# MLA scores from split fp32r operands instead of fp32 products, with the splitting placed two heads ahead

## The reference

```python
q_pe = apply_rope(q_pe, cos[:, :, None], sin[:, :, None])
k_pe = apply_rope(k_rope, cos, sin)
scale = (MLA_NOPE + MLA_ROPE) ** -0.5
...
s = (jnp.einsum('bqhd,bkhd->bhqk', qn, k_nope)
     + jnp.einsum('bqhd,bkd->bhqk', qp, k_pe)).astype(jnp.float32) * scale
...
p = masked_softmax(s, kpos[None, :] <= qpos[:, None])
return jnp.einsum('bhqk,bkhd->bqhd', p.astype(v.dtype), v)
```

## Time and profile before

| | |
|---|---|
| median of 3 runs | 1079.6 us (1079.23 to 1080.19) |
| the profiled execution's own time | 1080.06 us |
| its span | 1078.0 us |
| TensorE busy | 1058.9 us, 98% |
| VectorE busy | 634.5 us, 59% |
| ScalarE busy | 500.1 us, 46% |
| GpSimd busy | 101.7 us, 9% |

### The profile page before, as it was taken

The page is one execution under the profiler, slowest core; times in us unless marked ns, Lnnn a source line. Parts: engine busy times, 40 slices in busy tenths (PEclk is TensorE's granted clock), DMA queues, the critical chain, the costliest instruction groups (busy, mean ns, idle before and its releaser), DMA issues.

```text
span 1078.0 us, 14561 instructions
## 1 busy us (share of the span) xinstructions
PE 1058.9 (98%) x5706; PEld 906.8 (84%) x5706; DVE 634.5 (59%) x795; ACT 500.1 (46%) x620; POOL 101.7 (9%) x163
## 2 busy tenths in 40 slices
PE   8999999999999999999999999999999999999996
PEld 7889898888877888888888888888888888888885
DVE  4655765788765645556556545555655545655565
ACT  4646644776664544334334333433433433443434
POOL 2145100532203000000000000000000000000003
PEclk9999999999999999999999999999999999999999
DMA  9586562252335465655666656566666655656552
GB/s 332 165 209 198 180 211 85 73 196 78 94 103 157 157 195 179 191 182 192 192 195 195 188 187 186 183 192 192 195 194 189 189 183 185 191 192 195 194 196 78
DMA packets 89138, 190.44 MB, mean 177 GB/s; under 512 B 8758, under 2 KB 29836, under 8 KB 88716
## 3 DMA queue, kind: packets, MB, share of 16 engines
q1 hardware_dynamic: 88668, 189.41, 55.3%
q10 hardware_dynamic: 432, 0.52, 0.2%
HBM read 187.82 MB, written 2.10 MB: 176 GB/s over the span
## 4 chain that ended last, share of the span: by engine, by line
PE 92%; DVE 3%; ACT 2%; issue 1%; POOL 1%; DMA 0%; DVEq 0%; ACTq 0%
PE ps L1660 22%; PE ps L1266 14%; PE ps L1267 14%; PE ps L1270 14%; PE ps L1663 11%; PE ps L1533 2%; PE ps L1534 1%; PE ps L1537 1%; PE ps L1517 1%; PE ps L1492 1%; DVE w_lo L831 1%; PE ps L1331 1%; PE ps L1471 1%; PE ps L1518 1%; ACT w_hi L559 1%
## 5 line engine op out<-in xcount | busy, mean ns | idle before, releaser
L831 DVE TENSOR_TENSOR w_lo<-raw,w_hi 128x2048 fp32r<-128x2048 f32 (+4 forms) x198 | 402.6, 2036 | 354.7 <-ACT w_hi L566 287.8
L566 ACT ACTIVATE w_hi<-raw 128x2048 fp32r<-128x2048 f32 x119 | 228.1, 1917 | 396.3 <-PE ps L1270 200.8
L1660 PE MATMUL ps<-xT,w_hi 128*128 128x512 f32 x1024 | 279.5, 394 | 1.3 <-DVE h_sb L1035 1.0
L1660 PEld LDWEIGHTS ps<-xT,w_hi 128*128 128x128 f32 x1024 | 175.9, 189 | 26.1 <-issue 1.3
L1663 PEld LDWEIGHTS ps<-xT,w_lo 128*128 128x128 f32 x1024 | 157.1, 189 | 21.7
L1266 PE MATMUL ps<-w_hi,hidT 128*128 128x512 f32 x448 | 174.5, 390 | 0.0
L1267 PE MATMUL ps<-w_lo,hidT 128*128 128x512 f32 x448 | 174.4, 389 | 0.0
L1663 PE MATMUL ps<-xT,w_lo 128*128 128x256 f32 x1024 | 162.8, 281 | 0.0
L1270 PE MATMUL ps<-w_hi,hidT 128*128 128x512 f32 x448 | 138.1, 389 | 0.0
L559 ACT ACTIVATE w_hi<-raw 128x1024 fp32r<-128x1024 f32 (+3 forms) x75 | 103.8, 1391 | 72.0 <-PE ps L1270 41.4
L1270 PEld LDWEIGHTS ps<-w_hi,hidT 128*128 128x128 f32 x448 | 84.1, 188 | 17.6
(11 more groups left out here) (309 smaller groups left out, 1309.1 us busy)
## 6 DMA issues: line engine op xcount, KB each, us to landing
raw<-in_w_up SPq DMA_DIRECT2D x64, 1024.0 KB, 5.3
raw<-in_w_down SPq DMA_DIRECT2D x64, 1024.0 KB, 5.5
raw<-in_w_o SPq DMA_DIRECT2D x16, 1024.0 KB, 5.6
raw<-in_w_in SPq DMA_DIRECT2D x8, 1024.0 KB, 5.2
raw<-in_w_in SPq DMA_DIRECT2D x8, 816.0 KB, 4.4
raw<-in_w_in SPq DMA_DIRECT2D x6, 832.0 KB, 8.2
raw<-in_mla_w_uq SPq DMA_DIRECT2D x12, 256.0 KB, 4.2
raw<-in_mla_w_ukv SPq DMA_DIRECT2D x4, 512.0 KB, 5.4
```

The source lines that it names most:

```text
L566: act.activation(w_hi[:, j % SPLIT, :], raw[:, j % RAW, :], ACT.Copy).then_inc(hi_done, 1)
L831: return dve.tensor_tensor(dst, src, high.bitcast(F32), ALU.subtract)
L1660: pe.matmul(both, w_hi[:, slot, 512 * b + P * f:512 * b + P * f + P], xT[:, :, k0 + b, :], start=start and b == 0, stop=False)
```

## The change

The MLA scores use fp32r operands. For each head ScalarE copies `qnT` and `knT` to `qh` and `kh` (two places each, for even and odd heads), and VectorE subtracts, giving `qnL` and `knL`, which lie over `qnT` and `knT`. For each pair of heads, at the even one, the rotary queries get the layout of the NSA queries: `qs` holds a head's high part on one half of the partitions and its low part on the other. The rotary key stands on both halves already; it is now written as fp32r (`kpT`), and its low part is `kpl`. A group of scores is then five fp32r matmuls: three for the 128 features, two for the rotary ones. The new item `("m", i)` splits head i. Heads 0 and 1 stand around the GELU behind chunk 27, head i+2 directly behind slot i.

```diff
{DIFF}
```

More of the change, by code:

```diff
@@ L86 @@
     PLAN += [("w", _c)] + [(part, (_c + 1, half)) for half in range(2) for part in ("hi", "lo") if _c > CMP[0]]
-    PLAN += {CMP[1]: [("k", "rotary_k"), ("k", "rows")], CMP[2]: [("c", 0)], CMP[3]: [("k", "gelu")], A_IN[3]: [("k", "turn")]}.get(_c, [])
+    PLAN += {CMP[1]: [("k", "rotary_k"), ("k", "rows")], CMP[2]: [("c", 0)], CMP[3]: [("m", 0), ("k", "gelu"), ("m", 1)], A_IN[3]: [("k", "turn")]}.get(_c, [])
 _s = 0
@@ L149, in build @@
         KC_AT = YN_AT + 4 * 2 * 6 * T
+        assert e <= KC_AT
+        qh, kh, qs, kpl, e = seq(KC_AT - 4 * 9 * T, ("qh", [P, 2, T], F32R), ("kh", [P, 2, T], F32R), ("qs", [P, 2, 2, T], F32R),
+                                 ("kpl", [P, T], F32R))
         assert e <= KC_AT
@@ L715, in _ @@
                     m.then_inc(v_pad, 1)
+                elif kind == "m":
+                    if i >= 2:
+                        act.wait_ge(score_t, i - 1)
+                    act.wait_ge(qn_out, 4)
+                    act.wait_ge(kn_out, 4)
+                    act.activation(qh[:, i % 2, :], qnT[:, i, :], ACT.Copy)
+                    act.activation(kh[:, i % 2, :], knT[:, i, :], ACT.Copy).then_inc(mq_hi, 1)
+                    if i % 2 == 0:
+                        act.wait_ge(qp_out, 2)
+                        for e in range(2):
+                            r = slice(64 * e, 64 * e + 64)
+                            m = act.activation(qs[r, i // 2 % 2, e, :], qpT[r, i // 2, :], ACT.Copy)
+                        m.then_inc(mp_hi, 1)
                 elif kind == "c":
@@ L1078, in _ @@
                     m.then_inc(k_ok, 1)
+                elif kind == "m":
+                    dve.wait_ge(mq_hi, i + 1)
+                    low(qnL[:, i, :], qnT[:, i, :], qh[:, i % 2, :])
+                    low(knL[:, i, :], knT[:, i, :], kh[:, i % 2, :]).then_inc(mq_lo, 1)
+                    if i % 2 == 0:
+                        dve.wait_ge(mp_hi, i // 2 + 1)
+                        for e in range(2):
+                            r, other = slice(64 * e, 64 * e + 64), slice(64 - 64 * e, 128 - 64 * e)
+                            m = low(qs[other, i // 2 % 2, e, :], qpT[r, i // 2, :], qs[r, i // 2 % 2, e, :])
+                        m.then_inc(mp_lo, 1)
+                elif i == "rotary_k":
+                    dve.wait_ge(qp_out, 3)
+                    low(kpl[:, :], bank(6, T), kpT[:, :]).then_inc(kp_lo, 1)
                 elif i == "rows":
@@ L1469, in score @@
                         if kind == "mla":
-                            pe.matmul(o, qnT[:, h, q:q + P], knT[:, h, 0:c1 - c0], start=True, stop=False)
-                            m = pe.matmul(o, qpT[p0:p0 + 64, h // 2, q:q + P], kpT[p0:p0 + 64, 0:c1 - c0], start=False, stop=True)
+                            s = qs[:, h // 2 % 2, h % 2, q:q + P]
+                            pe.matmul(o, qh[:, h % 2, q:q + P], kh[:, h % 2, 0:c1 - c0], start=True, stop=False)
+                            pe.matmul(o, qh[:, h % 2, q:q + P], knL[:, h, 0:c1 - c0], start=False, stop=False)
+                            pe.matmul(o, qnL[:, h, q:q + P], kh[:, h % 2, 0:c1 - c0], start=False, stop=False)
+                            pe.matmul(o, s, kpT[:, 0:c1 - c0], start=False, stop=False)
+                            m = pe.matmul(o, s, kpl[:, 0:c1 - c0], start=False, stop=True)
                         else:
```

13 lines of the change are left out of this document (9 added, 4 removed).

## The result

The changed kernel takes **1086.9 us** in the median of its four runs (1084.43, 1086.71, 1087.06, 1087.41) against 1079.65 for the kernel before (1079.23 to 1080.19): ratio 1.0062, 95% interval [1.0050, 1.0074], so 7.2 us slower. In five more runs, in a later series, it took 1084.5 to 1086.9, median 1085.1, ratio 1.0055 [1.0041, 1.0069]. The forecast was 1081.8 us, range 1079.4 to 1084.6. The sign was right, the size wrong: the median is 2.3 us above the range, and that of the later series 0.5 us.

What follows compares the result with a forecast made beforehand. TensorE, busy 98% of the span, was taken as the bound. Stalls of 9.1 us against 6.9 us gained gave +2.2 us on the median of 1079.6: 1081.8 us forecast, range 1079.4 to 1084.6.

Steps and rivals of the forecast that it cites:

- The sign: Whole kernel: the change makes it slower, by a net +2.2 us.
- The scores: MLA heads on TensorE: ten fp32r matmuls take 1.15 us instead of 1.98, saving 6.6 us over eight heads.
- the switch behind heads 0 to 2: First fp32r matmul behind these heads' scores no longer takes 0.22 us instead of 0.12: 0.3 us saved.
- The four waits: TensorE stalls for VectorE's w_lo at chunks 29, 30, 31, 32: 0.75, 4.8, 1.85 and 1.7 us, 9.1 in all.
- rival 1: Clock falls to half in the 4.8 us stall at chunk 30, costing 1.7 us more: 1083.5 us; chance 0.19.
- On 64 partitions I take the same: VectorE's 64x256 rotary subtractions cost as much as 128x256 ones: 0.42 us long, 0.35 to the next.
- No gap inside the kernel is as long: Kernel before: no TensorE gap matches the 3.5 us after the last matmul before the clock fell; the new 4.8 does.
- the 1.7 us stop: TensorE's longest stop before, for w_lo, in the stretch 118 to 146 us; mean clock 1.00 there.
- (2) hidden: Small operations for heads 2, 4 and 6 finish before TensorE needs the chunk; all 6.9 us kept: 1072.7 us; chance 0.06.
- the written order ties the copies to the exponentials: Argument against hiding: ScalarE's copies for a head stand behind the exponentials of two heads before.
- (3) balance: Small operations nearer 0.27 us than 0.4 take about 2 us out of the four chains: 1079.8 us; chance 0.14.
- (4) dearer operations: Dearer small operations, or scores at 1.7 us instead of 1.15, add 2.2 us: 1084.0 us; chance 0.11.

Runs made afterwards that it cites:

- e7_fill3: Changed kernel with 36, 13 and 11 extra matmuls filling TensorE's waits at chunks 30, 31 and 32: 1083.09 us, ratio 1.0032.
- e2: Changed kernel with heads 2 to 7 not split, their scores using the operands of heads 0 and 1: 1075.78 us, ratio 0.9964.
- e6: Changed kernel with heads 2, 4, 6 split behind the next w_lo, head 1 behind chunk 29's, and chunk 30's w_lo ahead of the compressed keys' product: 1074.92 us.
- e15: The changed kernel again, unchanged, for a second profile: 1085.11 us, ratio 1.0055 to the kernel before.
- e1: Changed kernel with 36 extra matmuls filling TensorE's wait at chunk 30 only: 1086.34 us, ratio 1.0060.
- e10: Kernel of e6 with twelve extra matmuls in its wait at chunk 22: 1073.88 us, ratio 0.9943.
- e12: Kernel of e6 with extra matmuls in its waits at chunks 22, 29 and 31: 1074.49 us, ratio 0.9946.
- e14: Changed kernel with thirteen and eleven extra matmuls in the waits at chunks 31 and 32 only: 1083.76 us, ratio 1.0039.
- e9_again2: Kernel before the change, with VectorE making chunk 30's w_lo twice more, a lone wait of 4.53 us: 1085.87 us, ratio 1.0061.
- e3_fp32scores: Changed kernel with all splitting kept but the scores made as fp32 products again: 1089.67 us, ratio 1.0087.
- e8: Kernel before the change, with VectorE making chunk 30's w_lo once more, a lone wait of 2.20 us: 1083.83 us, ratio 1.0045.

## Why the prediction was wrong

**The scores: right.** 1.15 us per head forecast, 1.16 measured; with the switch behind heads 0 to 2 the whole gain was put at 6.9 us. The rows agree: the eight heads take 15.96 us in before (2.09 and seven times 1.98) and 9.37 now (1.25 and seven times 1.16), 6.6 less, and 0.3 for the switch.

**The four waits: right in place, releaser and order, 1.2 us short in size.** Forecast 0.75, 4.8, 1.85 and 1.7 us; the rows have 0.90, 4.98, 2.01 and 1.81. To these comes 0.16 each that the rows do not show: the idle time is counted from the modelled end of the last matmul (0.28 long), while without a wait the next one would start 0.12 behind it. In all 9.70 + 0.64 = 10.3 against 9.1. (For chunk 29 the prediction's own positions, 155.05 + 0.9 + 0.05 less 155.30, give 0.70 and not 0.75.) The mis-sized term is "On 64 partitions I take the same": I took 0.35 us to the next instruction for each of the rotary operations, and the pair takes 0.88 (166.67 to 167.55), after 0.1 in which VectorE waits for their copies. Four subtractions are 1.67 us (165.88 to 167.55) and not 1.40, and this 0.27 stands in each of the four chains: 1.1 of the 1.2. The subtraction of 128x256 itself was right (0.43 long, 0.34 to the next, forecast 0.42 and 0.35), and so was the copy (0.40 and 0.31). Net 3.5 us instead of 2.2: with this alone the time would be 1083.1, inside the range, as e7_fill3 is; so this is not what made the forecast miss.

**The clock: the step that failed.** The forecast's sum has nothing for it. It was rival 1, with a chance of 0.19 and 1.7 us for one fall at chunk 30; measured 3.8 us in the median (2.0 in the later series), and three falls in the one profile of a run at 0.993, the mean clock of four of the nine runs. The sentences that were wrong are "No gap inside the kernel is as long" and what they rest on: from the one fall in the trace of before (3.5 us behind the last matmul) I made a length that a gap must reach. The runs show falls in or up to 1.5 us behind waits of 4.98, 4.53, 3.31, 2.01, 1.82, 1.55 and 0.78 us. In the wait at chunk 30 the clock fell 2.1 us after the last matmul in one run of the changed kernel and 4.9 after it (164.64 to 169.58, from the 0.79 of the window 169 to 170) in another; behind the program's last matmul it took 2.5 us (e2, e6) to 4.9 us (e15). One example of a fall gives neither the shortest nor the longest time that a fall takes, and the window of full clock over the 1.7 us stop showed only that a wait of that length need not cause a fall. With that, waits of 2 us at chunks 31 and 32 were exposed as well, and I priced the clock for one wait only. By the rule of the Trainium skill that the prediction weighed (TensorE: Matmul & The Clock Gate, HAM oscillation — how this bites in real kernels), the fall is paid again at each wait that lets it come; the second profile of the changed kernel agrees (waits of 4.98, 2.01 and 1.80 us, three falls, 1.5 us each). The case that the section describes has waits of 3 to 5 us between the bursts; the runs here show that waits of 2.01, 1.55 and 0.78 us are exposed too, in part of the runs.

**The rivals.** (2) hidden, 1072.7: wrong for this order, but e6_best shows that it was a matter of order alone: its two best runs, both at 0.998, took 1073.1 and 1073.4. That "the written order ties the copies to the exponentials" was the right reason. (3) balance, 1079.8: wrong, the operations were dearer, not cheaper. (4) dearer operations, 1084.0: half right, by 1.2 of its 2.2 us; it and the clock came together, and the forecast had them as alternatives. Summed they are 1081.8 + 1.2 + 3.8 = 1086.8; but the 3.8 was read off the measured median, so this sum is no test. The tests are that e7_fill3, without falls, lands at 1083.1, and that each fall costs 1.5 us by positions.

## What to carry to other kernels

Work that another engine must do for a later step goes behind the conversion that the bound engine needs next, not between it and the results it waits for: moving one entry of the order turned +7 us into -3, two more into -5. A wait put into a saturated TensorE cost its length here and, in part or all of the runs, 1.5 to 1.7 us of half clock on top, and three waits cost it three times in one run; so a forecast should carry that term as a risk for every wait of a microsecond or two that a change adds. Where waits can't be avoided, matmuls into an unused bank during them are worth trying: they saved 2.0 to 3.8 us here, by the series that one compares with.

## What the runs showed of the hardware

- A dip of the granted clock (2.4 to 1.2 GHz) lasted 3.4 us (e1, e2, e10, e12, e14, e15) or 6.8 us (the first profile of the changed kernel, 167.0 to 173.8; e9_again2; e3_fp32scores at chunk 30). Only the part that falls on work costs: at half clock the fp32r matmuls follow at 0.213 us instead of 0.12, so 3.4 us of it cost 1.5.
- Whether a wait brings a dip differs from run to run of the same kernel (e8, 2.20 us: none in one run of five by the mean clock; e9, 4.5 us: in all five), and its start, counted from the last matmul, differs by 2.8 us between two runs at the same wait. Behind waits of 1.5 to 2 us it came 0.7 to 1.5 us after TensorE had begun again (e1, e2, e15).
- The mean clock of a whole run counts the dips, and also the time at half clock behind the last matmul, 3.9 to 6.3 us, which costs nothing. The profiled runs have 0.997 or 0.998 without a dip inside, 0.996 or 0.995 (e2) with one of 3.4 us, 0.995 with one of 6.8 (the changed kernel, e9) or with two (e1), and 0.993 with three (e15) or with one of each length (e3). So the number tells the dips of a run to within one.
- A VectorE subtraction of 64x256 takes as long as one of 128x256 (0.42 and 0.43 us), and the pair on different partitions took 0.88 us, 0.44 each, where those of 128x256 follow at 0.34 (the changed kernel, 165.88 to 167.55).
